# Turning the value blocks of an attention layer by VectorE squares and short-run stores instead of by TensorE transposes

## What is computed

```python
h = rms_norm(x, norm_pre) * (1 + scale) + shift           # scale, shift, gate from c @ ada_w
q = (h @ w_in[:, 0:2048]).reshape(b, s, 8, 2, 128)
k = (h @ w_in[:, 2048:4096]).reshape(b, s, 8, 2, 128)
v = (h @ w_in[:, 4096:6144]).reshape(b, s, 8, 256)
z =  h @ w_in[:, 6144:8192]
p = softmax(mask(q k^T * scale))                          # two maps for each head
attn = p[:, :, 0] - lam * p[:, :, 1]
o = rms_norm(attn @ v, subln) * (1 - lambda_init) * silu(z)
x = x + gate * rms_norm(o @ w_out, norm_post)
```

## Time and profile before

| what | value |
|---|---|
| median of three runs | 1907.08 us |
| the profiled execution, its own time | 1907.34 us |
| its span in the trace | 1905.5 us |
| TensorE busy (matmul) | 1866.0 us, 98% |
| VectorE busy | 1379.5 us, 72% |
| ScalarE / GpSimd busy | 810.1 us, 43% / 794.4 us, 42% |
| DMA engines, main queue | 76.4% of 16 engines' span |

### The profile page before, as it was taken

One profiled execution on the slowest core, in us unless ns is written; L12 is line 12 of the kernel. 1 busy time (PEld: TensorE's weight loads), 2 busy tenths in 40 slices (PEclk: granted clock), 3 DMA queues, 4 the chain that ended last, 5 costly groups with the idle time before them and its releaser, 6 DMA issues.

```text
span 1905.5 us, 26384 instructions
## 1 busy us (share of the span) xinstructions
PE 1866.0 (98%) x9072; PEld 1540.9 (81%) x9072; DVE 1379.5 (72%) x2028; ACT 810.1 (43%) x1516; POOL 794.4 (42%) x844
## 2 busy tenths in 40 slices
PE   4999999999999999999999999999999999999998
PEld 1488888888888888888888888888888888888886
DVE  3687888886655546787887877878778776569467
ACT  5633333333444433444443444444444445546452
POOL 2076565655644523344344434434443422116023
PEclk9999999999999999999999999999999999999999
DMA  9898898886674698786877778686777679657777
GB/s 354 253 313 279 274 297 278 284 290 232 214 267 160 237 356 263 225 250 192 253 229 227 235 216 252 198 254 212 232 240 221 213 228 291 207 186 257 258 240 265
DMA packets 394048, 473.16 MB, mean 248 GB/s; under 512 B 22614, under 2 KB 268476, under 8 KB 391228
## 3 DMA queue, kind: packets, MB, share of 16 engines
q1 hardware_dynamic: 393632, 471.43, 76.4%
q10 hardware_dynamic: 284, 0.05, 0.0%
HBM read 323.54 MB, written 147.86 MB: 247 GB/s over the span
## 4 chain that ended last, share of the span: by engine, by line
PE 93%; DVE 1%; DMA 1%; ACT 0%; issue 0%; SPq 0%; POOL 0%; DVEq 0%; POOLq 0%; ACTq 0%
PE ps L1752 30%; PE ps L1754 30%; PE ps L1753 30%; PE ps L1885 2%; PE ps L1861 1%; PE ps L1904 1%; PE ps L1721 0%; DMA ubf<-s_dr 0%; DMA z_dr<-cc 0%; PE ps L1833 0%; DVE ring L1310 0%; ACT h L1040 0%; DVE xt L1632 0%; DVE tB L1330 0%; DVE tB L1327 0%
## 5 line engine op out<-in xcount | busy, mean ns | idle before, releaser
L1752 PE MATMUL ps<-blk,ring 128*128 128x512 f32 x1524 | 603.3, 396 | 2.6 <-DVE blk L1357 1.9
L1754 PE MATMUL ps<-blk,ring 128*128 128x512 f32 x1524 | 594.6, 390 | 0.0
L1753 PE MATMUL ps<-blk,ring 128*128 128x512 f32 x1524 | 594.2, 390 | 0.0
L1752 PEld LDWEIGHTS ps<-blk,ring 128*128 128x128 f32 x1524 | 286.3, 188 | 66.0 <-issue 9.7
L1754 PEld LDWEIGHTS ps<-blk,ring 128*128 128x128 f32 x1524 | 286.0, 188 | 60.8
L1753 PEld LDWEIGHTS ps<-blk,ring 128*128 128x128 f32 x1524 | 286.5, 188 | 55.8
L1310 DVE TENSOR_TENSOR ring<-sums,ring 128x512 fp32r<-128x512 f32 x256 | 234.7, 917 | 95.5 <-ACT ring L1006 93.6
L836 POOL TENSOR_TENSOR sums<-raw 128x512 f32<-128x512 f32 x128 | 191.5, 1496 | 226.9 <-DVE ring L1310 206.0
L1006 ACT ACTIVATE ring<-sums 128x512 fp32r<-128x512 f32 x256 | 160.6, 628 | 179.3 <-PE ps L1754 175.6
L1310 DVE TENSOR_TENSOR ring<-raw,ring 128x512 fp32r<-128x512 f32 x192 | 179.2, 934 | 58.9 <-ACT ring L1006 58.5
L836 POOL TENSOR_TENSOR sums<-sums,raw 128x512 f32<-128x512 f32 x128 | 190.2, 1486 | 20.8 <-DVE ring L1310 14.3
(11 more groups left out here) (159 smaller groups left out, 3181.7 us busy)
## 6 DMA issues: line engine op xcount, KB each, us to landing
raw<-in_diff_w_in_dram SPq DMA_DIRECT2D x64, 1024.0 KB, 7.8
d_dr<-cc SPq DMA_DIRECT2D x124, 256.0 KB, 3.2
cc<-d_dr SPq DMA_DIRECT2D x124, 256.0 KB, 4.1
ubf<-s_dr SPq DMA_DIRECT2D x113, 256.0 KB, 5.0
ada<-in_ada_w_dram SPq DMA_DIRECT2D x88, 256.0 KB, 7.3
tb<-in_diff_w_out_dram SPq DMA_DIRECT2D x32, 512.0 KB, 5.5
t_dr<-tb SPq DMA_DIRECT2D x32, 512.0 KB, 4.9
ada<-in_ada_w_dram SPq DMA_DIRECT2D x32, 512.0 KB
```

What stands on the lines that cost most here:

```text
L1752: MM(dst, a_hi, b_hi, start=start, stop=False, skip_group_check=True)
L1753: MM(dst, a_hi, b_lo, start=False, stop=False, skip_group_check=True)
L1754: return MM(dst, a_lo, b_hi, start=False, stop=stop, skip_group_check=True)
```

## The change

TensorE no longer turns the v blocks: its `v_turn` is gone. VectorE gets a `v_turn` in its place, one instruction for each block, after the `take` of that block: it turns each 32x32 square of the 128x512 block by itself, from `cc` into PSUM bank 7. After it, partition 32a+i holds, in columns 32g to 32g+31, the 32 channels from 32a on of token 32g+i. The split into `ev` and `cc_low` is as before. The stores finish the turning: each of the two tiles is stored by four DMAs of 32 partitions, in runs of 32 floats (128 bytes), where one DMA with runs of 128 floats (512 bytes) stood. `v_dr` ends up with the same contents in the same layout. The counts on the semaphores `stored` follow the larger number of v stores (`parts_stored`).

```diff
+        def parts_stored(n):
+            h, k = divmod(n, PARTS_IN)
+            v = 2 * 16 * (P // SIDE)
+            return h * (v + 32 * (PARTS_IN - 1)) + (v + 32 * (k - 1) if k else 0)
...
                     if part == 2:
-                        dst = v_dr[h * SEQ + half * HALF:h * SEQ + (half + 1) * HALF].rearrange("(t p) s d -> p t s d", p=P)
-                        sp.dma_start(dst[:, :, s, m * P:(m + 1) * P],
-                                     src.rearrange("p (t d) -> p t d", t=HT).bitcast(F32)).then_inc(stored[o], 16)
+                        dst = v_dr[h * SEQ + half * HALF:h * SEQ + (half + 1) * HALF, s]
+                        for d in range(0, P, SIDE):
+                            sp.dma_start(dst[:, m * P + d:m * P + d + SIDE].rearrange("(g i) j -> i g j", i=SIDE),
+                                         src[d:d + SIDE].rearrange("i (g j) -> i g j", j=SIDE).bitcast(F32)).then_inc(
+                                             stored[o], 16)
...
                 if part == 2:
-                    act.wait_ge(vt_mm, 4 * h + o + 1)
+                    act.wait_ge(vt_ok, 4 * h + o + 1)
                     A(ev[:, o], ps[:, VX], ACT.Copy).then_inc(post_hi, 1)
...
+            def v_turn(n):
+                i, pi = divmod(n, NP)
+                h, o = head_part(i)[0], AT[pi]
+                if h or o:
+                    dve.wait_ge(post_d, 12 * h + o if o else 12 * (h - 1) + 4)
+                dve.wait_ge(ev_d, 3 * GP + NP * (i - GP) + pi + 1)
+                V.transpose(ps[:, VX], cc[:, buffer_of(i, BLOCK[pi])]).then_inc(vt_ok, 1)
...
+                if n - 1 >= NA and (n - 1) % NP in BLOCK and head_part((n - 1) // NP)[1] == 2:
+                    v_turn(n - 1)
...
-            def v_turn(i, pi):
-                h, _ = head_part(i)
-                b, o = BLOCK[pi], AT[pi]
-                pe.wait_ge(*read_out(i, pi))
-                if h or o:
-                    pe.wait_ge(post_d, 12 * h + o if o else 12 * (h - 1) + 4)
-                for t in range(HT):
-                    last = TR(ps[:, VX, t * P:(t + 1) * P], cc[:, buffer_of(i, b), t * P:(t + 1) * P], ident[:, :])
-                last.then_inc(vt_mm, 1)
```

More of the change, by code:

```diff
@@ L16 @@
 CHUNK = 64
+SIDE = 32
 def build(nc, x, c, ada_w, ada_b, norm_pre, norm_post, w_in, w_out, lq1, lk1, lq2, lk2, subln, out):
@@ L294, in build @@
         d_ld = [sem(f"d_ld{i}") for i in range(CCR)]
-        post_hi, post_d, post_p, vt_mm = sem("post_hi"), sem("post_d"), sem("post_p"), sem("vt_mm")
+        post_hi, post_d, post_p, vt_ok = sem("post_hi"), sem("post_d"), sem("post_p"), sem("vt_ok")
         stored = [sem(f"stored{i}") for i in range(4)]
@@ L421, in build @@
                  for n in uses if n[0] >= GP}
+        def parts_stored(n):
+            h, k = divmod(n, PARTS_IN)
+            v = 2 * 16 * (P // SIDE)
+            return h * (v + 32 * (PARTS_IN - 1)) + (v + 32 * (k - 1) if k else 0)
         def stored_block(i, b):
-            return stored[ORDER.index(b)], 32 * (i - GP + 1)
+            return stored[ORDER.index(b)], parts_stored(i - GP + 1)
         read = {}
@@ L537, in load_qk @@
                     for e in range(4):
-                        sp.wait_ge(stored[e], (h * 4 + 3) * 32)
+                        sp.wait_ge(stored[e], parts_stored(h * PARTS_IN + 3))
                 if a > 0:
@@ L551, in load_v @@
                     for e in range(4):
-                        sp.wait_ge(stored[e], (h * 4 + 1) * 32)
+                        sp.wait_ge(stored[e], parts_stored(h * PARTS_IN + 1))
                 if a > 1:
@@ L561, in load_z @@
                     for e in range(4):
-                        sp.wait_ge(stored[e], (h * 4 + 4) * 32)
+                        sp.wait_ge(stored[e], parts_stored(h * PARTS_IN + 4))
                 if a > 0:
@@ L1121, in post_high @@
                 if i > GP:
-                    act.wait_ge(stored[o], 32 * (i - GP))
+                    act.wait_ge(stored[o], parts_stored(i - GP))
                 src = cc[:, buffer_of(i, b)]
                 if part == 2:
-                    act.wait_ge(vt_mm, 4 * h + o + 1)
+                    act.wait_ge(vt_ok, 4 * h + o + 1)
                     A(ev[:, o], ps[:, VX], ACT.Copy).then_inc(post_hi, 1)
```

## The result

The changed kernel takes 1975.51 us in the median of four runs (1974.3 to 1979.12). The kernel before, beside it, takes 1907.3 us. The ratio is 1.036, with a 95% interval of 1.0341 to 1.0377: 68 us slower. The sign was forecast and the time lies in the range, but the forecast loss was 34 us, half of what came.

The account below looks back on a forecast made before the run. TensorE, busy 98% of the span, was taken to bound the kernel. A late load costing 4.5 us a head, 31.5 us in seven heads, and 2.4 us in the first adds 34 us to 1907: 1941 us, range 1910 to 1985.

Parts of the forecast that it names:

- TensorE, -0.45 us a block: On TensorE, dropping the four transposes of each turned block saves 0.45 us, 14.4 us for 32 blocks.
- VectorE at nothing: VectorE's 32 new turns, 0.65 us each, were costed at nothing in the sum: busy, not full.
- rival D: VectorE at 1.31 us a turn: at most 10 us on top, 1951; inside the range, no chance of its own.
- The queue, 0.55 us an issue: SyncE queue: 30 issues take 16.5 us, so the load of the first-half block is issued 4.7 us late.
- The spare: Slack of the load of the first-half block before VectorE and TensorE must wait: 0.7 us together, once in each head.
- the old stretch: SyncE queue before the change, from the v store of `P7` to the load of the first-half block: 11.8 us.
- The DMA engines, "15.1 us, just under the 16.5 us of issuing": Engine work in that queue stretch: three v blocks 9.9 us plus six other transfers 5.2 us, so issuing sets the pace.
- what queues behind the longer stores: Loads of weights, q, k and v behind the v stores on SyncE's queue: users come late enough, costed at nothing.
- rival A: Small packets are dear, up to 29.5 ns each, so the DMA engines decide: 2027, anything from 1975 up; chance 0.14.
- for engines that are as good as full: Term of 0.5 us added to the landing of the late load in each head, for nearly full DMA engines.
- The clock as a rival (C): TensorE's clock falls after its stall, one slot a head at half speed: 2.9 us a head, 1961; chance 0.15.
- The forecast stall: TensorE stands still before `weighted` in each head, about 4.5 + 1.8 = 6.3 us.

## Why the prediction was right in sign and half in size

**TensorE, -0.45 us a block.** The transposes are gone, and the stream is unbroken. What it brings is less than 14.4 us: 10.9 with no load late, 7.6 with the old order of the queue.

**VectorE at nothing.** One turn takes 0.723 us, not 0.65. Of the 3.5 us that remain between 10.9 and 14.4, 1.2 may be its price; rival D is far off.

**The queue, 0.55 us an issue.** Right: 24 and 6 issues with large runs took 16.1 us (16.5 forecast), late all through. Right, too, is the place where it hurts. The spare was 1.1 us a head, not 0.7, and the old stretch 12.1 us, not 11.8.

**The DMA engines, "15.1 us, just under the 16.5 us of issuing".** This step failed. The packet was well estimated, 13.4 ns for 12.8. But the stretch of the head shown held 18.5 us of work (19.0 on average over the seven heads). Its packets, all queues together:

```profile
DMA packets 15534, 3.84 MB, mean 196 GB/s; under 512 B 11864, under 2 KB 15217, under 8 KB 15532
```

Of the 11864 below 512 bytes, 11350 have 128 bytes and took 9.7 us of each engine, by the single packets of the trace. The other 8.8 us are 3335 packets of 512 bytes (6.3 us), 315 of 2 KB (2.1 us) and 514 of 4 bytes (0.3 us), where the prediction had 5.2 us for five and a half transfers. What it left out are mainly transfers issued before the stretch and not yet done when it began at 930.24: the loads of v, q and k and of a first-half block. They were issued between 925.3 and 928.4, behind a load of weights of 1 MB, and landed 6.0 to 7.2 us later. The prediction named the loads of v, q and k as what queues behind the longer stores, and costed them at nothing because their users come late enough. They take engines all the same. In the prediction's own formula for rival A, the engines decide from (16.5 - 8.8) us / 709 packets for each engine = 10.9 ns on, not from 14.7, and the packet is above that. So the first half of rival A was true at a price far below its 29.5 ns. The term of 0.5 us "for engines that are as good as full" should have been 4.7 us a head, by the two kernels with eight stores.

**The clock as a rival (C) with 0.15.** This step failed as well. The forecast stall was 6.3 us and the trace of before had the fall of the clock in it; the cost follows from the stall and belonged in the likeliest case. It was sized at 2.9 us a head; it is 2.0 at most.

The sum: 4.5 us a head were forecast, 9.3 came. The queue alone gives 2.9 (16.1 - 12.1 - 1.1), the small packets 4.7, the clock 1.7 to 2.0, together 9.3 to 9.6. That the kernel with eight 512-byte stores took 1940.8 us, just what was forecast for the whole change, is chance: its queue cost less than forecast, and its clock, which fell too (83.8 us from `aT_lo` to the next `P2`), made up for it.

## What to carry to other kernels

When a queue is late throughout, only one waiter shows it at first, so look at the whole queue: list all that crosses the DMA engines in the stretch, also what was issued before it and what nobody waits for, and take the larger of the issues' time and the engines' time. Put the load that somebody waits for ahead of stores that nobody waits for, before making the stores more numerous; a row of issues costs by what stands behind it and waits, and small packets make the row itself longer. If the forecast has TensorE standing still for longer than it did, and the trace shows its clock fall somewhere after such a stop, the lower clock belongs in the sum.

## What the runs showed of the hardware

- One VectorE square transpose of 128x512 float32 into PSUM takes 0.72 us (711 to 727 ns, 32 of them).
- A packet of 128 bytes into DRAM takes 13.4 ns of one DMA engine, one of 512 bytes 28.5 ns, with no other work on the engines; in stores of 32 partitions, whose pace the issues set, the 512 bytes took 35.6 ns.
- An issue of the SyncE queue takes longer when the DMA engines are full: 0.49 to 0.54 us alone, 0.78 us in a run of four in the changed kernel, and 2.9 us in the median for a store of 2048 small packets directly behind another.
- After a stop of 7.28 us TensorE's granted clock was 0.50 from 955 to 960 us, and 1.00 again from 962 us on.
